# Moving half of the low weight parts to GpSimd and reordering ScalarE's queue in the expert stage of a mixed LRU and mixture-of-experts kernel

## What is computed

```
cond = silu(c);  sh1, sc1, g1, sh2, sc2, g2 = split(cond @ ada_w + ada_b)
hn = rmsnorm(x, norm1_g) * (1 + sc1) + sh1
y  = rglru_mixer(hn)                      # in-projection, causal conv, gates, linear scan, out-projection
x  = x + g1 * y
hn = rmsnorm(x, norm2_g) * (1 + sc2) + sh2
probs = softmax(hn @ router_w + router_b) # 16 experts in 4 groups; best group, top 2 in it
out_e = (silu(hn @ w_gate[e]) * (hn @ w_up[e]) * gate) @ w_down[e]     # 1024 -> 256 -> 1024
x  = x + g2 * (sum over a token's two experts of out_e)
return rmsnorm(x, final_norm_g)
```

## Time and profile before

| what | value |
|---|---|
| median of three runs | 1349.78 us |
| profiled execution / its span | 1347.12 us / 1345.5 us |
| TensorE (PE) busy | 81% |
| VectorE (DVE) busy | 66% |
| ScalarE (ACT) busy | 44% |
| GpSimd (POOL) busy | 42% |
| mean granted TensorE clock | 0.934 of full |

### The profile page before, as it was taken

One profiled execution on the slowest core, in us unless ns is written; L12 is line 12 of the kernel. 1 busy time (PEld: TensorE's weight loads), 2 busy tenths in 40 slices (PEclk: granted clock), 3 DMA queues, 4 the chain that ended last, 5 costly groups with the idle time before them and its releaser, 6 DMA issues. The chain is left out here.

```text
span 1345.5 us, 20384 instructions
## 1 busy us (share of the span) xinstructions
PE 1092.1 (81%) x4860; PEld 874.6 (65%) x4861; DVE 883.4 (66%) x1249; ACT 592.9 (44%) x890; POOL 571.2 (42%) x603
## 2 busy tenths in 40 slices
PE   1459999999999993799999925968778788887882
PEld 0347778778778772688888714756656666666661
DVE  6983676666667663556677664657667667777762
ACT  1554666766766763322222121343444444454430
POOL 0786625625525510024767661223333343434432
PEclk9999999999999997899999956978888899999996
DMA  8536324424433322913555393476567756667631
GB/s 303 178 82 209 101 95 128 155 98 129 144 109 116 122 79 76 333 63 125 189 191 216 126 341 115 130 266 231 187 215 252 261 209 233 234 222 252 208 127 63
DMA packets 146298, 232.60 MB, mean 173 GB/s; under 512 B 34240, under 2 KB 101824, under 8 KB 145616
## 3 DMA queue, kind: packets, MB, share of 16 engines
q1 hardware_dynamic: 111248, 128.20, 29.0%
q0 software_dynamic: 23632, 62.49, 12.9%
q10 hardware_dynamic: 11376, 41.42, 9.3%
HBM read 177.45 MB, written 91.31 MB: 200 GB/s over the span
## 5 line engine op out<-in xcount | busy, mean ns | idle before, releaser
L1618 PE MATMUL pl<-w_hi,e_xh 128*128 (+1 forms) x312 | 132.2, 424 | 13.9 <-DVE w_lo L1303 8.2
L1303 DVE TENSOR_TENSOR w_lo<-w_raw,w_hi 128x1536 f32 x60 | 102.9, 1757 | 45.7 <-ACT w_hi L1419 25.1
L1173 PE MATMUL po<-wo_hi,b_yh 128*128 128x512 f32 x256 | 104.7, 409 | 26.7 <-DVE wo_lo L989 26.7
L1640 PE MATMUL po<-w_hi,e_ah 128*128 (+1 forms) x156 | 71.5, 458 | 67.4 <-DVE w_lo L1303 53.2
L1619 PE MATMUL pl<-w_lo,e_xh 128*128 (+1 forms) x312 | 125.5, 402 | 0.0
L1620 PE MATMUL pl<-w_hi,e_xl 128*128 (+1 forms) x312 | 125.4, 402 | 0.0
L1321 POOL DMA_INDIRECT out_dram<-e_ob,e_idx_o x39 | 42.3, 1084 | 192.4 <-DVE e_ob L1545 165.7
L543 DVE SCALAR_TENSOR_TENSOR XB<-xu,conv_w,XB 128x512 f32<-128x512 f32 x96 | 91.5, 953 | 43.2 <-ACT XB L413 39.5
L1419 ACT ACTIVATE w_hi<-w_raw 128x1536 f32 x60 | 86.0, 1479 | 75.3 <-PE po L1642 34.1
L636 PE MATMUL px<-hT_hi,wx_hi 128*128 128x512 f32 x256 | 102.2, 399 | 5.1 <-DVE wx_lo L477 5.1
L636 PE MATMUL pg<-hT_hi,wg_hi 128*128 128x512 f32 x256 | 104.2, 407 | 0.0
(11 more groups left out here) (270 smaller groups left out, 2782.0 us busy)
## 6 DMA issues: line engine op xcount, KB each, us to landing
e_xg<-hn_slots ACTq DMA_DIRECT2D x40, 512.0 KB
e_xa<-x_slots ACTq DMA_DIRECT2D x39, 512.0 KB, 3.6
stg<-in_ada_w_dram POOLq DMA_DIRECT2D x32, 512.0 KB, 4.2
w_raw<-in_moe_w_gate_dram SPq DMA_DIRECT2D x32, 384.0 KB
w_raw<-in_moe_w_up_dram SPq DMA_DIRECT2D x32, 384.0 KB
n_ada<-in_ada_w_dram SPq DMA_DIRECT2D x16, 512.0 KB, 5.1
n_x<-in_x_dram SPq DMA_DIRECT2D x16, 512.0 KB, 3.3
hn_slots<-in_x_dram SPq DMA_DIRECT2D x16, 512.0 KB, 4.9
```

The source lines that it names most:

```text
L1173: nc.tensor.matmul(po[u][:, hcols], yh[u][:, tok], wo_hi[:, k, hcols], start=(k == 0), stop=False)
L1303: nc.vector.tensor_tensor(w["lo"][:, ds(off + q * QW, QW)], raw1[q][:], w["hi"][:, ds(off + q * QW, QW)].bitcast(F32), ALU.subtract).then_ ...
L1618: nc.tensor.matmul(gu[:], xh[:, tok], hi, start=(k == 0), stop=False)
L1640: nc.tensor.matmul(dst, ah[:, tok], hi, start=(k == 0), stop=False)
```

## The change

Four edits:

1. ScalarE's step: `high_a` comes right behind `square`, `load_x` behind it, `index_out` behind `high_x` and in front of `index_acc`.
2. The low parts of the odd quarters (q = 1 and 3) are made by GpSimd, behind `root` in its step; VectorE keeps q = 0 and 2. This holds from the second expert on; the first expert's parts are made as before.
3. The sends of the last tiles: one tile at s = 15 instead of two, `root(15)` directly behind it, then two tiles.
4. The record scatters of the last two tiles count on `sent_x` (now 6 DMAs, 96) and no longer on `sent`, so that ScalarE issues its first token load without them; SP waits for `sent_x` too.

```diff
             def send_rec(it):
                 for c in range(TOPK):
-                    pool.indirect_dma_start(dr["rec"], rows(pos[:, c, it:it + 1]), rec[:, c, it], None).then_inc(sent[it % RING], 16)
+                    pool.indirect_dma_start(dr["rec"], rows(pos[:, c, it:it + 1]), rec[:, c, it], None)\
+                        .then_inc(sent[it % RING] if it < NT - 2 else sent_x, 16)
...
                 shift(s - 1)
+                if s == NT - 2:
+                    send(s - 5)
                 if s >= NT - 2:
-                    send(2 * s - NT - 3)
-                    send(2 * s - NT - 2)
+                    send(s - 4)
             root(NT - 1)
-            send(NT - 4 + 1)
+            send(NT - 4)
+            send(NT - 3)
...
             all_sent(sp)
+            sp.wait_ge(w["sent_x"], 96)
             sp.wait_ge(w["tabled"], 1)
...
-                eng.wait_ge(w["sent"][r], 160 if r < RING - 2 else 144)
-
-        def low_w(eng, b, dues=None):
+                eng.wait_ge(w["sent"][r], 160 if r < RING - 2 else 112)
+
+        def low_w(eng, tensor_tensor, b, odd, dues=None):
...
-                    for q in (2 * part, 2 * part + 1):
-                        eng.wait_ge(w["hi_done"], NQ * e + (q + 1))
-                        eng.nop(nofuse=True)
-                        nc.vector.tensor_tensor(w["lo"][:, ds(off + q * QW, QW)], raw1[q][:],
-                                                w["hi"][:, ds(off + q * QW, QW)].bitcast(F32),
-                                                ALU.subtract).then_inc(w["lo_done"][q % 2], 1)
+                    q = 2 * part + odd
+                    eng.wait_ge(w["hi_done"], NQ * e + (q + 1))
+                    eng.nop(nofuse=True)
+                    tensor_tensor(w["lo"][:, ds(off + q * QW, QW)], raw1[q][:],
+                                  w["hi"][:, ds(off + q * QW, QW)].bitcast(F32),
+                                  ALU.subtract).then_inc(w["lo_done"][odd], 1)
...
+            low = lambda b: low_w(pool, nc.gpsimd.tensor_tensor, b, 1)
             all_sent(pool)
-            pool.wait_ge(w["sent_x"], 32)
+            pool.wait_ge(w["sent_x"], 96)
...
             with pool.Fori(2, nless) as i:
                 scatter_out(i)
                 scatter_acc(i + 1)
                 root(i + 1)
+                low(i + 2)
...
-            act.wait_ge(w["sent_x"], 32)
+            act.wait_ge(w["sent_x"], 96)
...
             with act.Fori(LEAD, nless) as i:
                 square(i)
-                index_out(i)
+                high_a(i + 1)
                 load_x(i + 1)
-                high_a(i + 1)
                 tanh(i + 2)
                 high_x(i + 3)
+                index_out(i)
                 index_acc(i + 1)
                 high_w(i + 2)
...
-            low = lambda b, dues=None: low_w(dve, b, dues)
+            low = lambda b, dues=None: low_w(dve, nc.vector.tensor_tensor, b, 0, dues)
             act_product(0)
             low_x(1)
-            for done in w["lo_done"]:
-                dve.wait_ge(done, 2)
+            dve.wait_ge(w["lo_done"][0], 2)
```

More of the change, by code:

```diff
@@ L1338, in root @@
                 nc.gpsimd.tensor_tensor(rstd[:], root0[:], part[:], ALU.mult).then_inc(rstd_ready, 1)
+            low = lambda b: low_w(pool, nc.gpsimd.tensor_tensor, b, 1)
             all_sent(pool)
-            pool.wait_ge(w["sent_x"], 32)
+            pool.wait_ge(w["sent_x"], 96)
             nc.gpsimd.memset(ab_eps[:, D:], 32.0 * EPS ** 0.5).then_inc(consts, 1)
             pool.wait_ge(w["tabled"], 1)
+            pool.wait_ge(w["lo_done"][1], 2)
             nless = blocks_less(pool)
+            low(0)
             pool.wait_ge(consts, set_up)
@@ L1347, in expert_gpsimd @@
             root(0, True)
+            low(1)
             scatter_out(0)
@@ L1350, in expert_gpsimd @@
             root(1)
+            low(2)
             scatter_out(1)
@@ L1353, in expert_gpsimd @@
             root(2)
+            low(3)
             with pool.Fori(2, nless) as i:
@@ L1360, in expert_gpsimd @@
             root(nless + 1)
+            low(nless + 2)
             scatter_out(nless + 1)
@@ L1458, in expert_scalar @@
             index_acc(0, True)
-            index_out(0, True)
             high_w(1)
@@ L1462, in expert_scalar @@
                 square(b, b == 0)
-                if b > 0:
-                    index_out(b)
+                high_a(b + 1)
                 load_x(b + 1)
-                high_a(b + 1)
                 tanh(b + 2)
                 high_x(b + 3)
+                index_out(b, b == 0)
                 index_acc(b + 1)
@@ L1481, in expert_scalar @@
             square(nless)
+            high_a(nless + 1)
+            load_x(nless + 1)
+            tanh(nless + 2)
             index_out(nless)
-            load_x(nless + 1)
-            high_a(nless + 1)
-            tanh(nless + 2)
             index_acc(nless + 1)
@@ L1488, in expert_scalar @@
             square(nless + 1)
+            high_a(nless + 2)
+            load_x(nless + 2)
             index_out(nless + 1)
-            load_x(nless + 2)
-            high_a(nless + 2)
             square(nless + 2)
```

## The result

The changed kernel takes 1375.24 us (median of 4 runs, 1374.50 to 1380.27); the kernel before, run beside it, takes 1350.74. The ratio is 1.0181 (95% interval 1.0156 to 1.0205): slower by about 24 us, where 26 us less were forecast. In the profiled executions the span goes from 1345.5 to 1373.6 us.

The account below looks back on a forecast made before the run. The chain through ScalarE and VectorE, not TensorE, bounds the expert blocks' 12.4 us cycles. Savings 4.4 + 22.9 + 3 - 4 = 26.3 us from 1347.1 give 1320.8; plus 2.7 for the median, forecast 1323, range 1300 to 1343.

Parts of the forecast that it names:

- the slack that the shorter cycle leaves: ScalarE's queue behind the moved output-index copy in the expert blocks: weight copies and `index_acc` could wait, at no cost.
- The shared port: VectorE's and GpSimd's low parts exclude each other but run at different times: adds 0, upper bound 97 us lost.
- Late landings: Late `e_ab` scatter landings lengthened two two-block-expert cycles beside two weight loads; one load starting later saves 3 us together.
- The six two-block cycles: Cycles of two-block experts, 86.6 us in all, where q2 stays VectorE's first operation: unchanged except 3 us saved.
- GpSimd's price: GpSimd's 128x1536 low-part subtraction takes 3.6 us (2.4 to 5.4), from T + 5.6 to T + 9.2, T ending an `e_ab`.
- Hidden: GpSimd's low part pushes the next output scatter by 1.2 us, but the `e_ab` scatter is due later: no cost.
- the one-block expert: The one cycle where TensorE wants q1 before GpSimd, starting behind root, has made it: +4 us, once.
- The ordinary cycle: The other 28 expert-block cycles, 11.7 us each, fall to 10.9 us: 22.9 us saved.
- The hand-over: Passage into the expert stage: root 6.5 us earlier, less 2.1 for SP's wait, so weights come 4.4 us earlier.
- rival 1: VectorE's `e_ob` is held by GpSimd's low part, +2.4 us in some 27 cycles: about 1389 us; chance 0.10.
- Rival 4: The cycle moves to another wait, GpSimd's chain of 11.2 us a cycle: no gain, 1345 us; chance 0.08.

Follow-up runs that it names:

- 8 columns: The changed kernel with GpSimd's low part only 8 columns wide instead of 1536: 1365.03 us, 1.0116 of the kernel before.
- the pairs above: Changed kernel, GpSimd's low part 8 columns against full: 1.0116, 1.0181. VectorE's low parts waiting for the square, without and with GpSimd's low parts: 1.0032, 1.0123.

## Why the prediction was wrong

**The step that failed** is the one that priced the queue behind the moved copy at nothing: the weight copies "and `index_acc`, have the slack that the shorter cycle leaves". `index_acc` had stood in front of `high_w` before, too, and the slack was taken from cycles where its landing was on time. Its waits grew from 19.5 to 66.0 us, and taking it from in front of `high_w` gives back 42 us, more than the whole loss of 24.

**The shared port** was weighed against the wrong partner. "They miss each other. That by itself adds 0" is true of the two subtractions (GpSimd's start at T + 6.3 to 8.8 in ordinary cycles, VectorE's at T + 0.5 to 0.8), but GpSimd's scatter at T + 0.83 was left out. I put VectorE's low part at T + 1.05, from cycles of the kernel before; with one operation in its branch instead of two it starts earlier, and that moved it across the scatter's start. The trace of the kernel before had five such cycles already (the low part at T + 0.65 to 0.68, the scatter 2.43 to 2.46 us), one of them right before the wait of the earlier trace rows, which I had put down to weight loads. Its timeline (T = 1053.34):

```profile
1054.03 3.43 DVE L1303 TENSOR_TENSOR w_lo<-w_raw,w_hi 128x1536 f32 x2 [0.68 <-issue]
...
1054.17 2.46 POOL L1314 DMA_INDIRECT x_slots<-e_ab,e_idx_a  x1 [1.58 <-issue]
```

That GpSimd's move causes the earlier start is shown (5 starts against 14 to 17); why it does is not. It is not simply the shorter branch: a memset ahead of both low parts, without the move, also brings the start before T + 0.80 in 11 and in 16 cycles. The Trainium skill (SBUF — State Buffer, "SBUF: two separate sides") states that GpSimd can't write the descriptors of a DMA that it issues while VectorE runs an operation in a two-port mode. Of `tensor_tensor`, the operation of the low parts, the same page of the Trainium skill ("Who interferes with whom") says that a probe did not show it stalling a DMA, and infers why. The traces differ from that: 2.35 us against 0.98, and all of the 119 cases. So the first rule, on which I did not draw, names the right partner, GpSimd's DMAs; the second would have let the change pass. The memset has no input, and which mode it ran in no row shows.

**Late landings** were a matter of two cycles and 3 us in the prediction, and put down to two weight loads. Without the weights' bytes the waits stay at 61.4 us; without the row loads' bytes as well they are 20.4. The new order had moved just these two loads next to the scatter. The six two-block cycles, "-3", came to +16.5.

**GpSimd's price** was right: 3.50 us against 3.6. But it began at about T + 7 instead of T + 5.6, with 2.0 to 3.7 us under "issue" ahead of it instead of 1.2, and a root that starts at T + 3.1 to 3.4 behind a stretched scatter. "Hidden" failed: where it runs past T, the next scatter starts at T + 1.3 to 2.6 (13 of 35; none with 8 columns). By the pairs above this and all else on GpSimd cost 9 to 12 us, most of them in the one-block expert. That was the right place with the wrong size, +11.5 instead of +4: not one part but two, in a row, behind a root that itself was late; 9 to 10 us of it by the same pairs.

**The ordinary cycle** at 10.9 was about right for those that nothing holds: 11.0 over 23 of them, 11.2 without the last two.

**The hand-over**, -4.4, has the right size in the runs with the sends alone: -4 us (0.5 to 7 by the interval). Its route is not shown. The profiled execution was 3.8 us behind before the stage began (VectorE's third-last L901 at 745.41 against 741.65), so I count from there. The root comes 6.0 us earlier (6.5 forecast). But SP's record loads began 6.0 us behind the end of the last send (815.81 to 821.84), where 3.4 were taken, and the weights leave 131.5 us after L901 instead of 129.7 (130.1 with the sends alone): later, not 4.4 us earlier. Of the 5.8 us at the first `e_ab`, 2.4 are left at the `e_ab` of the earlier trace rows with the sends alone (149.2 against 151.6 us), and none in the changed kernel (151.7).

**The rivals.** `e_ob` was never held: 1281 ns before and after, so rival 1 had the sign but not the mechanism, and its 0.10 was all that I had for slower. Rival 4's chain of 11.2 us on GpSimd did not set the pace: ten of the 28 other cycles are shorter than that. What was missing is a rival that follows GpSimd's scatter: who holds it up, which loads are ahead of it, and who stands behind its landing.

## What to carry to other kernels

When work moves to GpSimd, list what GpSimd issues besides it: here its scatters were held by VectorE's subtraction of two SBUF tensors, and a start 0.1 us earlier decided who was first. An index copy that waits for a landing goes behind everything that does not need it; here this is worth 42 us in one kernel and 11 in another. A change of four edits is several predictions: the order (8 us) and the sends (4 us) gained, less than forecast for the order, and the sum was lost in what had been priced at nothing. An unusual row of the old trace (here a scatter of 2.46 us) is to be explained before its wait is priced.

## What the hardware did that I had not expected

- GpSimd's indirect scatter takes 0.98 us alone. When VectorE's subtraction (1.76 us) has begun 0.05 us or more before it, it takes up to 2.56 us and ends 0.85 us after the subtraction does (119 cases in twelve traces); begun 0.04 us before, the subtraction holds nothing.
- VectorE's two low parts in a row at T + 0.66 hold it no longer than one: 2.4 to 2.5 us. A memset and a subtraction in a row hold it through both, up to 2.75 us.
- From issue to landing the same scatter takes 2.1 to 9.5 us with two 512 KB loads beside it, 2.1 to 5.0 without their bytes and the weights'.
- GpSimd takes 3.50 us for a 128x1536 subtraction from SBUF, VectorE 1.76.
